# One-core two-block transformer kernel: gate bias as 128-row products, the dt product in split passes, the first norm from the feature copy, and the feed-forward gating spread over its block

## The reference

```python
# first block, for each of 2 layers
h = rms_norm(x, norm1_g[l])                              # x / sqrt(mean(x^2) + eps) * gain
q, k, v, gu, gv = split(h @ w_in[l])                     # 2048 x 3584 (28 column groups of 128)
attn = banded_window_attention(rope(norm(q)), rope(norm(k)), v, sink[l])
vn = layer_norm(gelu(gv)).reshape(B, nc, 128, 8, 128)    # 2 chunks of 128 tokens, 8 heads
f = einsum('hpq,bcqhd->bcphd', w_s, vn) + b_s.T[None, None, :, :, None]   # the "spatial gate"
sgu = gelu(gu) * f
x = x + concat(rms_norm(attn), rms_norm(sgu)) @ w_o[l]
a = depthwise_conv3(rms_norm(x) @ w_up[l]) + conv_b      # 2048 x 11264, 3 taps along the tokens
g, u = split(a)
x = x + (silu(g) * u) @ w_down[l]                        # 5632 x 2048

# second block
q, k, v, z, xbc, dt_raw = split(rms_norm(x) @ w_in_2)    # the last 16 columns are dt_raw
dt = softplus(dt_raw + dt_bias)
# ... attention, state-space mixer, output product, cross attention, relu^2 feed-forward
```

## Time and profile before

| | |
|---|---|
| time, 3 runs | 3450.89 us median (3449.79 to 3451.9) |
| the profiled execution | 3451.57 us, of which the span of the profile 3449.7 us |
| mean granted TensorE clock | 0.991 of full speed |
| PE busy | 3395.1 us, 98% of the span |
| DVE busy | 2049.6 us, 59% |
| ACT busy | 1617.2 us, 47% |
| DMA | 600.52 MB, mean 174 GB/s |

### The profile page before, as it was taken

One profiled execution on the slowest core, in us unless ns is written; L12 is line 12 of the kernel. 1 busy time (PEld: TensorE's weight loads), 2 busy tenths in 40 slices (PEclk: granted clock), 3 DMA queues, 4 the chain that ended last, 5 costly groups with the idle time before them and its releaser, 6 DMA issues.

```text
span 3449.7 us, 44217 instructions
## 1 busy us (share of the span) xinstructions
PE 3395.1 (98%) x18022; PEld 2900.8 (84%) x18022; DVE 2049.6 (59%) x1888; ACT 1617.2 (47%) x1640; POOL 111.5 (3%) x80
## 2 busy tenths in 40 slices
PE   7999999999999999999999999999999999999999
PEld 7988888888888988888888888889989888888887
DVE  4756565556556655565655666466777555555555
ACT  4554544444444464544444445337654544444443
POOL 0110000000000111000000000010012000000000
PEclk9999999999999999999999999999999999999999
DMA  6335555555554434555555554434354355555554
GB/s 247 135 111 184 192 185 183 183 184 188 187 183 177 148 121 161 184 189 186 182 183 186 187 185 174 147 123 147 135 184 170 143 188 187 190 188 189 194 184 170
DMA packets 85670, 600.52 MB, mean 174 GB/s; under 512 B 9344, under 2 KB 11424, under 8 KB 13616
## 3 DMA queue, kind: packets, MB, share of 16 engines
q1 hardware_dynamic: 84112, 593.53, 48.3%
q0 software_dynamic: 1440, 5.24, 0.4%
HBM read 596.64 MB, written 2.10 MB: 174 GB/s over the span
## 4 chain that ended last, share of the span: by engine, by line
PE 87%; DVE 9%; issue 1%; ACT 1%; DMA 1%; DVEq 0%; SPq 0%; ACTq 0%
PE ps L473 21%; PE ps L475 21%; PE ps L474 21%; PE ps L441 6%; PE ps L442 5%; PE ps L443 5%; DVE w_lo L1615 4%; PE ps L482 2%; DVE x_stream L1695 1%; DVE up_conv L1882 1%; DVE up_conv L1885 1%; PE ps L662 1%; PE ps L661 1%; DMA x_stream<-in_x 0%; PE ps L565 0%
## 5 line engine op out<-in xcount | busy, mean ns | idle before, releaser
L1615 DVE TENSOR_TENSOR w_lo<-w_raw,w_hi 128x2048 fp32r<-128x2048 f32 x560 | 1280.5, 2296 | 540.1 <-ACT w_hi L1107 539.5
L1107 ACT ACTIVATE w_hi<-w_raw 128x2048 fp32r<-128x2048 f32 x560 | 1068.5, 1913 | 1080.7 <-DMA w_raw<-in_weights 1080.7
L473 PE MATMUL ps<-w_hi,actb_hi 128*128 128x512 f32 x1920 | 751.5, 391 | 12.1 <-DVE w_lo L1615 12.1
L474 PE MATMUL ps<-w_hi,actb_lo 128*128 128x512 f32 x1920 | 747.3, 389 | 0.0
L475 PE MATMUL ps<-w_lo,actb_hi 128*128 128x512 f32 x1920 | 747.3, 389 | 0.0
L441 PE MATMUL ps<-act_hi,w_hi 128*128 128x256 f32 x1728 | 503.6, 291 | 24.2 <-DVE w_lo L1615 10.6
L442 PE MATMUL ps<-act_lo,w_hi 128*128 128x256 f32 x1728 | 493.6, 286 | 0.0
L443 PE MATMUL ps<-act_hi,w_lo 128*128 128x256 f32 x1728 | 493.3, 285 | 0.0
L473 PE MATMUL ps<-w_hi,h_hi 128*128 128x512 f32 x1216 | 476.6, 392 | 3.2 <-DVE h_lo L1895 3.2
L475 PE MATMUL ps<-w_lo,h_hi 128*128 128x512 f32 x1216 | 473.3, 389 | 0.0
L474 PE MATMUL ps<-w_hi,h_lo 128*128 128x512 f32 x1216 | 473.3, 389 | 0.0
(11 more groups left out here) (309 smaller groups left out, 2744.7 us busy)
## 6 DMA issues: line engine op xcount, KB each, us to landing
w_raw<-in_weights SPq DMA_DIRECT2D x560, 1024.0 KB, 4.8
x_features<-in_xT SPq DMA_DIRECT2D x4, 512.0 KB, 8.6
x_stream<-in_x SPq DMA_DIRECT2D x1, 2048.0 KB, 15.8
mem_sb<-in_mem POOLq DMA_DIRECT2D x4, 512.0 KB, 5.1
out_x<-x_stream SPq DMA_DIRECT2D x4, 512.0 KB, 2.8
w_s_sb<-in_w_s POOLq DMA_DIRECT2D x2, 512.0 KB, 10.1
consts_sb<-in_consts POOLq DMA_DIRECT2D x1, 686.5 KB, 8.8
consts_sb<-in_consts POOLq DMA_DIRECT2D x1, 576.0 KB, 12.1
```

The lines of the kernel that those rows point to most:

```text
L473: mm(o, a_hi, hi, start=first and c == 0, stop=False)
L474: mm(o, a_lo, hi, start=False, stop=False)
L1107: A(w_hi[:, s], w_raw[:, s], ACT.Identity).then_inc(hi_done, 1)
L1615: tt(w_lo[:, s], w_raw[:, s], hi_of(w_hi[:, s]), ALU.subtract).then_inc(w_ready, 1)
```

## The change

It has five parts. (1) The bias of the spatial gate is cleared to 128 rows and added first, by one product of 128 rows and 256 columns per head; 24 products per layer in place of 32. (2) The dt product is made of split weights like all others: 48 products in `fp32r` with 128 stationary columns (those past the 16 give rows that nobody reads), and ACT and DVE split the small weights. (3) The first norm's sums come from squares of the feature copy: four squares on ACT, seven additions on POOL, a sum by PE (`total_pairs`) and a factor row made on DVE by `inverse_root`; the wait for the token copy goes to the first addition to the residual, and `x_stream` is loaded last. The parameters beyond the first 16 columns are issued after `x_fm` and ahead of the constants. (4) Piece 0 is loaded and split in two halves. (5) In the feed-forward, the second half's taps go to the second and third down piece, the product to the fourth, and `hidden_hi` and `hidden_lo` into the next block. After the last block's up pieces the order is: taps, product one piece later, `hidden_lo` in the fourth.

```diff
@@ sync
+            half = PIECE // 2
+            sp.dma_start(w_raw[:, 0, 0:half], weights[0, :, 0:half]).then_inc(half_in, 16)
+            sp.dma_start(x_fm[:, 0:4], x_parts[:, 0:4]).then_inc(x_in[0], 16)
+            sp.dma_start(w_raw[:, 0, half:], weights[0, :, half:]).then_inc(raw_in[0], 16)
+            for j in range(1, 4):
+                sp.dma_start(x_fm[:, 4 * j:4 * j + 4], x_parts[:, 4 * j:4 * j + 4]).then_inc(x_in[j], 16)
+            for s in range(1, W_SLOTS):
                 sp.dma_start(w_raw[:, s], weights[s]).then_inc(raw_in[s], 16)
-                if s == 1:
-                    sp.dma_start(xs[:], x.rearrange("(b p) d -> p b d", p=P)).then_inc(x_tokens_in, 16)
+            sp.dma_start(xs[:], x.rearrange("(b p) d -> p b d", p=P)).then_inc(x_tokens_in, 16)
@@ gpsimd
-            pool.dma_start(prm1[:], params1).then_inc(prm_in, 16)
+            pool.dma_start(prm1[:, 0:KC], params1[:, 0:KC]).then_inc(gains_in, 16)
             pool.wait_ge(x_in[3], 16)
+            pool.dma_start(prm1[:, KC:], params1[:, KC:]).then_inc(prm_in, 16)
             pool.dma_start(cst[:], consts).then_inc(consts_in, 16)
...
+            for i in range(7):
+                pool.wait_ge(first_squares, (i + 1) // 2 + 1)
+                if i:
+                    pool.wait_ge(x_summed, i)
+                G.tensor_tensor(sqa[:], sqa[:] if i else sq_x[:, 0:2], sq_x[:, 2 * i + 2:2 * i + 4],
+                                ALU.add).then_inc(x_summed, 1)
@@ tensor
                     pe.wait_ge(consts_in, 3 * 16)
+                    total_pairs(7, SU0)
                 else:
                     opening(P0, W0, A0, D0, lambda: x_quarter(3, D0, A0 + 8))
-                factor_row(l)
+                    factor_row(0)
...
                     for h in range(8):
+                        both = ps[:, 4 + h // 2, h % 2 * T:(h % 2 + 1) * T]
+                        mm(both, ident[:, h:h + 1].to_broadcast([P, P]), over(bst, TB), start=True, stop=False)
                         for kb in range(TB):
-                            o = ps[:, 4 + h // 2, h % 2 * T + kb * P:h % 2 * T + (kb + 1) * P]
-                            mm(o, vnt[:, kb, h], wst[:, h], start=True, stop=False)
-                            last = mm(o, ident[0:8, h:h + 1].to_broadcast([8, P]), bst[0:8, :], start=False, stop=True)
+                            last = mm(both[:, kb * P:(kb + 1) * P], vnt[:, kb, h], wst[:, h], start=False, stop=kb == 1)
...
-                for part, acts in enumerate(A_IN):
-                    for c in range(KC):
-                        last = mm(ps[0:16, 6, 0:T], wdt_sb[:, c], acts[:, c].bitcast(F32),
-                                  start=part == 0 and c == 0, stop=part == 1 and c == KC - 1)
+                for c in range(KC):
+                    hi, lo = (w[:, c * SSM_HEADS:c * SSM_HEADS + P] for w in (wdt_hi, wdt_lo))
+                    mm(ps[:, 6, 0:T], hi, act_hi[:, c], start=c == 0, stop=False)
+                    mm(ps[:, 6, 0:T], hi, act_lo[:, c], start=False, stop=False)
+                    last = mm(ps[:, 6, 0:T], lo, act_hi[:, c], start=False, stop=c == KC - 1)
@@ scalar
             split(1, 1)
-            act.wait_ge(x_tokens_in, 16)
             for j in range(4):
-                x_squared(0, j, 1)
+                A(sq_x[:, 4 * j:4 * j + 4], x_fm[:, 4 * j:4 * j + 4], ACT.Square).then_inc(first_squares, 1)
+            act.wait_ge(prm_in, 16)
...
-                        elif first and k == 2:
+                        elif k == (2 if first else 0):
                             hidden_hi(b - 1, 1 - par)
...
-                        elif k == 2:
+                        elif last and k == 2:
                             hidden_hi(b, par)
@@ vector
                     tick(P0, 0)
                     tick(P0 + 1, 1)
-                    x_mean(0)
-                    x_inverse(0)
-                    x_diagonal(0)
-                x_row(l, rstd)
+                    tick(P0 + 2, 2)
+                    dve.wait_ge(prm_in, 16)
+                    step(inverse_root(0, ps[:, 7, 0:T], rstd, D))
...
-                        elif first and k == 2:
+                        elif k == (2 if first else 1):
                             hidden_lo(b - 1, 1 - par)
...
                         if k == 1:
-                            taps(b, 1)
+                            taps(b, 1, 0)
+                        if k == (1 if last else 2):
+                            taps(b, 1, 1)
+                        if k == (2 if last else 3):
                             gated_hidden(b)
-                        elif k == 2:
+                        if last and k == 3:
                             hidden_lo(b, par)
```

More of the change, by code:

```diff
@@ L1168, in x_root_of @@
                 A(tk[:, 1, 0:2], tk[:, 0, 0:2], ACT.Sqrt).then_inc(x_root, 1)
-            split(0, 0)
-            act.wait_ge(prm_in, 16)
+            half = PIECE // 2
+            act.wait_ge(half_in, 16)
+            A(w_hi[:, 0, 0:half], w_raw[:, 0, 0:half], ACT.Identity).then_inc(half_hi, 1)
+            act.wait_ge(gains_in, 16)
             for j in range(4):
@@ L1175, in _ @@
                 prep(act_hi, x_fm, range(4 * j, 4 * j + 4), lambda c: prm1[:, C_N1 + c:C_N1 + c + 1])
+                if j == 0:
+                    act.wait_ge(raw_in[0], 16)
+                    A(w_hi[:, 0, half:], w_raw[:, 0, half:], ACT.Identity).then_inc(hi_done, 1)
             split(1, 1)
-            act.wait_ge(x_tokens_in, 16)
             for j in range(4):
-                x_squared(0, j, 1)
+                A(sq_x[:, 4 * j:4 * j + 4], x_fm[:, 4 * j:4 * j + 4], ACT.Square).then_inc(first_squares, 1)
+            act.wait_ge(prm_in, 16)
             def tick(p, s):
@@ L1192, in _ @@
                     tick(P0 + 1, 1)
-                    x_root_of(0)
-                for m in range(2, G1):
+                    tick(P0 + 2, 2)
+                    root_of(0)
+                for m in range(2 if l else 3, G1):
                     tick(P0 + m, m % 4)
@@ L1323, in up, with step1 @@
                             copy(b, 1, p + 8)
-                def step1(b, par, first=False):
+                def step1(b, par, first=False, last=False):
                     p = F0 + UP1 + (b - 1) * (UP1 + DOWN)
@@ L1486, in piece2 @@
                 steps(m)
+            act.wait_ge(wdt_in, 16)
+            A(wdt_hi[:, 0:256], wdt_sb[:], ACT.Identity)
+            A(wdt_hi[:, 256:], wdt_sb[:, 0:112], ACT.Identity).then_inc(wdt_hi_done, 1)
             for m in range(2, 16):
@@ L1737, in _ @@
             V.memset(soft[:, 1, 0, 0:1], 0.0).then_inc(added, 1)
-            split(0, 0)
-            dve.wait_ge(prm_in, 16)
+            V.memset(bst[:], 0.0).then_inc(bias_cleared, 1)
+            half = PIECE // 2
+            dve.wait_ge(half_hi, 1)
+            tt(w_lo[:, 0, 0:half], w_raw[:, 0, 0:half], hi_of(w_hi[:, 0, 0:half]), ALU.subtract).then_inc(half_ready, 1)
+            dve.wait_ge(gains_in, 16)
             for j in range(4):
                 dve.wait_ge(x_in[j], 16)
+                if j == 1:
+                    dve.wait_ge(hi_done, 1)
+                    tt(w_lo[:, 0, half:], w_raw[:, 0, half:], hi_of(w_hi[:, 0, half:]), ALU.subtract).then_inc(w_ready, 1)
                 prep(4 * j, A_IN, lambda c: x_fm[:, c], range(4 * j, 4 * j + 4), lambda c: prm1[:, C_N1 + c:C_N1 + c + 1])
@@ L1873, in _, with taps @@
                 col = lambda b, c, half, t: prm1[:, bass.ds(M0 + C_CONV + b * 32 + (2 * c + half) * 4 + t, 1)]
-                def taps(b, half):
+                def taps(b, half, t):
                     dst, bank = (ga, ua)[half], 4 + 2 * half
-                    src = lambda c, t: ps[:, bank + c // 2, c % 2 * T + t:c % 2 * T + t + T - 1]
+                    src = lambda c: ps[:, bank + c // 2, c % 2 * T + t:c % 2 * T + t + T - 1]
                     for c in range(4):
-                        if c % 2 == 0:
+                        if t == 0 and c % 2 == 0:
                             dve.wait_ge(conv_base, 2 * U0 + 4 * b + 2 * half + c // 2 + 1)
-                        last = stt(dst[:, c, 1:T], src(c, 0), col(b, c, half, 0), dst[:, c, 1:T], ALU.mult, ALU.add)
-                    step(last)
-                    for c in range(4):
-                        last = stt(dst[:, c, 0:T - 1], src(c, 1), col(b, c, half, 2), dst[:, c, 0:T - 1], ALU.mult, ALU.add)
-                    last.then_inc(conv_done, 1)
+                        out = dst[:, c, 1 - t:T - t]
+                        last = stt(out, src(c), col(b, c, half, 2 * t), out, ALU.mult, ALU.add)
+                    if t == 0:
+                        step(last)
+                    else:
+                        last.then_inc(conv_done, 1)
                 def gated_hidden(b):
@@ L1924, in _ @@
                     if k == 5:
-                        taps(0, 0)
+                        taps(0, 0, 0)
+                        taps(0, 0, 1)
                 step1(1, 1, True)
```

120 lines of the change are left out of this document (68 added, 52 removed).

## The result

The changed kernel takes 3410.2 us (median of 4 runs, 3408.66 to 3411.1), against 3451.39 in the runs of the kernel before that were made with them. The profiled execution took 3410.91 us, its span is 3409.0, 40.7 less than before.

A forecast was written before the change was run, and what follows sets the result against it. PE, busy for 98% of the span, was taken to bound the kernel. 27.3 + 7.9 + 17.1 - 10.4 - 3.1 - 0.7 = 38.1 us less gave 3412.8 us, range 3402 to 3424.

The forecast's parts named there:

- spatial gate, both layers: Gate stage: without alternating 8-row and 128-row products, 26.4 us a layer becomes 12.8 at full clock; 27.3 us less in both.
- dt product: The dt product: 48 rounded products at 0.12 us, 5.8 us in place of 13.6; 7.9 us less.
- blocks 1 to 9, with the 18 changes to the up pieces: Feed-forward: PE's wait for a late DVE split, 0.95 us a block, goes 18 times; 17.1 us less.
- last block, stop: Last feed-forward block: `h_lo` moves behind an addition and a split, so PE waits longer; 5.2 us more a layer, 10.4 in both.
- last block, clock behind the stop: After the last block's 7.0 us wait: clock 0.50 for about 3.1 us, losing 1.55; 3.1 us more for two.
- opening: Opening: the split for piece 2 waits for constants and starts 0.3 us later, PE's sum takes two products; 0.7 us more.
- the other reasons: Spatial gate rival: accumulation or spread column, not rows, keeps products at 0.42 us; 6.3 us back, 3419 us, chance 0.12.
- later waits that I had named: Feed-forward rival: the 0.95 us wait passes to the second up piece's split or `h_hi`; 17.1 back, 3430, chance 0.04.
- the bound of 5: Upper bound on the loss at half clock after the last block's waits; the lower bound was 0 us.
- halving piece 0 costs nothing: Opening: PE begins some 3 us sooner, but pieces 0 and 1 end long before piece 2 is ready, so worth nothing.
- The two others: Opening, constants' landing: 3.4 us later for the parameter transfer ahead of them, 1.2 sooner because `x_fm` lands sooner.
- The lower bound: Opening: if the constants are never late, piece 2 follows piece 1; 8 us less.

The follow-up runs named there:

- e4: Changed kernel with the spatial gate's 32 alternating products of the kernel before, but the bias product over all 128 rows; 3411.2 us (one run).
- e5: Changed kernel, its order of gate products kept, but the wide bias product over 8 rows in place of 128; 3423.4 us (one run).
- e7: Changed kernel with the whole feed-forward order of the kernel before; 3416.5 us, ratio 0.9897 to the kernel before.
- e1: Changed kernel, last feed-forward block's half ordered as before (taps, product in second down piece, `h_lo` in third); 3399.0 us, ratio 0.9842 to the kernel before.
- e8: Changed kernel with piece 0 loaded by one transfer and split whole; 3408.7 us, ratio 0.9873 to the kernel before.
- e12: Changed kernel, parameters beyond column 16 issued behind the three constants, ACT's wait for them behind its splits of pieces 2 to 4; 3408.6 us.
- e2: Changed kernel, DVE's wait for the constants and ACT's for the parameters moved behind their splits of pieces 2, 3 and 4; 3405.5 us.
- e3: Changed kernel with the edits of e1 and e2 together; 3393.4 us, ratio 0.9828 to the kernel before.

## Why the prediction was right, step by step

By distances from start to start in the two traces:

| term | forecast | measured |
|---|---|---|
| spatial gate, both layers | -27.3 | -27.2 |
| dt product | -7.9 | -8.2 |
| blocks 1 to 9, with the 18 changes to the up pieces | -17.1 | -17.6 |
| last block, stop | +10.4 | +10.2 |
| last block, clock behind the stop | +3.1 | +4.6 |
| opening | +0.7 | +2.4 |
| second block behind the dt product | 0 | -3.4 |
| the rest, mostly layer 1 | 0 | -1.5 |
| sum | -38.1 | -40.7 |

- **Gate.** Term and reason hold. e4 excludes the other reasons, and e5 shows that both halves of the cost, the 0.2 us a change and the fall of the clock, come with the 8 rows.
- **dt product, blocks 1 to 9.** Both held. The dt product had taken 13.9 us and not the 13.6 of the working. From the first token piece to the last down product ahead of the last block it is 816.1 us before (240.40 to 1056.47) and 807.3 after (229.18 to 1036.52), 8.7 less, and 8.9 less in layer 1. None of the later waits that I had named took over, and e7 brings the 18 stops back. The last `h_lo` ends 11 us into the up stage, as said (511.3, from the change at 500.2).
- **Last block.** The stop was right to 0.1 us a layer, and e1 takes it away again. The clock behind it was sized too small: half clock lasts to about 1049, over 5 us behind the restart, where I had taken the 3.1 of the opening. From the restart to PE's next stop it is 2.4 and 2.2 us more than before. It lies inside the bound of 5, and e1 confirms it by its 7.5 and 7.3.
- **Opening.** The step that failed is that halving piece 0 costs nothing. The features behind it land 1.7 us later (e8), the constants are issued only then, and they were this opening's bound. Their own transfers take as long either way (the last, 15.9 us from issue to landing in the changed kernel and 16.1 in e8), so it is the issue that what SyncE loads first holds back. The two others were near: the features land 1.1 us sooner with piece 0 whole (12.08, against 13.14 in the kernel before), forecast 1.2; the parameters ahead of the constants cost 2.2 to 2.4 us (e12), forecast 3.4. So the constants are in at 31.3 in place of 30.5, piece 2 starts 1.1 later, the half clock behind the stop lasts to 38.4 in place of 35.7, which is 0.8 more, and the sum by PE costs 0.43, as forecast. The 2.4 is known to about 1 us, since the gate is reached at 215.7 to 217.9 in seven traces with this opening. The lower bound, 8 less with the constants never late, was wrong as well: in e2 the constants hold up nothing, and the opening is 3.6 us ahead of the changed kernel's, so only 1.2 ahead of the one before; POOL's sums and the norm's factor are the next bounds.
- **What I did not forecast.** The granted clock in the second block, where the kernels run the same products, was worth 3.4 us to the changed kernel, and in e1 and e3 most of it is gone. It is no merit of the change: nothing was edited there, and the clock can differ so without an edit. The total came out 2.6 us below the forecast because this and layer 1 (4.9) outweighed the two losses that were sized too small (3.2). That the two nearly cancel is luck.

## What to carry to other kernels

A product of few rows between products of 128 costs more than itself: price the change of rows on both sides, and look at the granted clock of the stage even where PE is busy throughout. When work is spread over a loop's body, look at the last pass by itself: what the next pass covers has no cover there, and the remedy is to fill a gap in which the late engine waits, not to reorder what is all due at the same time. A wait that hides two others is worth only the distance to the next of them, and an engine that was free while DVE idled may not be once DVE is busy.

## What the runs showed of the hardware that I had not expected

- A change between products of 8 and of 128 rows costs 0.2 us in either direction at full clock (e5: 0.62 and 0.64 against 0.43 and 0.44), and a stage of such products falls to half clock with PE busy all the time (6.00 of 6 us), while the same stage with 128 rows keeps 1.00 (e4, changed kernel).
- POOL's addition of 128x512 takes 1.3 us alone and up to 3.16 beside DVE's 128x2048 subtraction, which itself goes from 2.29 to 3.37 (e2).
- Half clock comes and goes in one and the same program: at the same place, ahead of any edit, the mean is 1.00 in the changed kernel and 0.57 in e4, at equal busy time. In the second block, where nothing was edited, the same products take 1258.3 us in the changed kernel, 1261.0 in e1 and 1261.8 in the kernel before.
